# A memory tile moved from the router's stage to the end of the experts, and both norms there computed from one round of sums

## The reference

```python
h2 = modulate(x, norm2_g[l], sh2, sc2)
moe = hier_moe(h2.reshape(b * s, d), w_rg[l], b_rg[l], w_re[l], b_re[l],
               w1[l], w3[l], w2[l]).reshape(b, s, d)
x = x + g2[:, None, :] * moe
return rms_norm(x, norm_f_g)            # end of the first block
...
for i in range(DEPTH_2):                # the second block
    h = rms_norm_2(x, norm_w[i])
    ...                                 # GLA or S5 branch of h
    k, v = jnp.split(mem_n @ w_kv, 2, axis=-1)   # in memory_attention
```

## Time and profile before

| | us |
|---|---|
| median of 3 runs | 1678.35 |
| lowest, highest | 1676.72, 1678.55 |
| the profiled execution | 1676.78 |
| its span, first to last instruction | 1675.0 |
| PE busy in the span | 1566.1 (93%) |
| DVE busy | 578.7 (35%) |
| ACT busy | 321.9 (19%) |
| POOL busy | 54.0 (3%) |

### The profile page before, as it was taken

How to read it: one execution, slowest core, us unless ns; L and a number is a source line. 1 busy time by engine, 2 the same in 40 slices (tenths; PEclk the granted TensorE clock), 3 DMA queues, 4 the chain that set the end, 5 groups by cost and what they waited for, 6 DMA issues and landing times. The chain is left out here.

```text
span 1675.0 us, 20622 instructions
## 1 busy us (share of the span) xinstructions
PE 1566.1 (93%) x8428; PEld 917.0 (55%) x8428; DVE 578.7 (35%) x958; ACT 321.9 (19%) x547; POOL 54.0 (3%) x125
## 2 busy tenths in 40 slices
PE   5999998999999999994999999988999899699997
PEld 2485654444344444442445887547777775388843
DVE  2445323111111111113202111215999999720000
ACT  2222101111111111111200201003333343230000
POOL 0000000000000000000000000001111111000000
PEclk8999999999999999997999999998999999799999
DMA  9444647899999999993232242342333333124330
GB/s 402 169 157 188 257 200 318 339 422 422 422 422 422 422 422 422 422 410 130 107 144 101 101 151 101 146 156 94 146 114 113 115 148 129 63 101 151 151 151 25
DMA packets 46024, 371.59 MB, mean 222 GB/s; under 512 B 5888, under 2 KB 10368, under 8 KB 11408
## 3 DMA queue, kind: packets, MB, share of 16 engines
q1 hardware_dynamic: 45824, 369.75, 55.0%
q10 hardware_dynamic: 144, 1.05, 0.2%
HBM read 369.73 MB, written 1.05 MB: 221 GB/s over the span
## 5 line engine op out<-in xcount | busy, mean ns | idle before, releaser
L1228 PE MATMUL ps<-ring,x_gathered 128*64 128x512 f32 x1024 | 225.2, 592 | 0.9 <-DVE x_gathered L1296 0.9
L1911 PE MATMUL ps<-hT,ring 128*128 128x256 f32 x768 | 174.7, 386 | 1.9 <-PEq L113 1.9
L1416 PE MATMUL ps<-ring,zT 128*128 128x512 f32 x384 | 165.5, 592 | 0.0
L1911 PEld LDWEIGHTS ps<-hT,ring 128*128 128x128 f32 x768 | 146.0, 192 | 29.9 <-issue 10.4
L1228 PEld LDWEIGHTS ps<-ring,x_gathered 128*64 128x64 f32 x1024 | 73.6, 137 | 146.6 <-issue 146.6
L1305 DVE TENSOR_TENSOR act_slots<-gate,ps 64x512 f32<-64x512 f32 x32 | 22.1, 690 | 378.6 <-ACT gate L1267 378.6
L1416 PEld LDWEIGHTS ps<-ring,zT 128*128 128x128 f32 x384 | 72.9, 190 | 90.1 <-issue 89.9
L1251 PE MATMUL ps<-ring,act_turned 128*64 128x512 f32 x512 | 116.9, 598 | 0.0
L1529 PE MATMUL ps<-hT,ring 128*128 128x256 f32 x512 | 111.9, 380 | 0.0
L2086 PE MATMUL ps<-uT,ring 128*128 128x256 f32 x512 | 111.0, 379 | 0.0
L1529 PEld LDWEIGHTS ps<-hT,ring 128*128 128x128 f32 x512 | 96.8, 190 | 16.0 <-issue 3.1
(11 more groups left out here) (446 smaller groups left out, 1676.9 us busy)
## 6 DMA issues: line engine op xcount, KB each, us to landing
ring<-in_experts SPq DMA_DIRECT2D x192, 1024.0 KB, 15.8
ring<-in_weights SPq DMA_DIRECT2D x75, 2048.0 KB, 7.5
b_raw<-in_s_b SPq DMA_DIRECT2D x16, 128.0 KB, 7.4
c_raw<-in_s_c SPq DMA_DIRECT2D x16, 128.0 KB, 7.2
x<-in_x ACTq DMA_DIRECT2D x1, 1024.0 KB, 5.3
mix_room<-in_mem SPq DMA_DIRECT2D x1, 1024.0 KB, 17.2
rows_b_g<-in_rows SPq DMA_DIRECT2D x1, 1024.0 KB, 19.3
out<-x SPq DMA_DIRECT2D x2, 512.0 KB, 2.7
```

Source lines behind the costliest of these rows:

```text
L1228: last = pe.matmul(h_ps[rows, :], xg[:, f, :], w[:, kk, m, :], start=(f == 0), stop=(f == KD - 1))
L1416: last = pe.matmul(self.bank(n, t), self.zT[:, 8 * kb + kk, t * P:(t + 1) * P], w[:, kk, :], start=(first and kk == 0), stop=(self.ends(i) ...
L1911: last = pe.matmul(out[:, f, :], w[:, kk, (2 * h + f) * P:(2 * h + f + 1) * P], rhs[:, kk, :], start=(kk == 0), stop=(kk == KD - 1))
```

## The change

M3 leaves `FRONT` and the router's stage and becomes tile `T_END_FIRST` (24), the number that it had. It is loaded at the end of the experts, in front of the next layer's first two tiles, and its two halves are computed in `stage_first_end`: one and a half of them ahead of the transposes, the rest behind. ACT copies them to `vm` there. The next layer's third tile is now loaded in that layer. In the router's stage the second expert's tiles wait for A10, M2 and A11.

The end of the first block works by halves of 128 tokens, and DVE reads the experts' sum from PSUM. For each half DVE forms x and x times the first norm's gain (`xg`), ACT sums the squares of both, and POOL gets both factors from the two sums: with m = s/1024 + 1e-6, `keep_by` is 1/sqrt(m), and `turn_by` is 1/sqrt(sg/1024 + 1e-6 m), where sg is the sum of squares of `xg`. `xg` times `turn_by` is turned by PE for the next layer, `xg` times `keep_by` is the new x.

```diff
-         "O0", "O1", "M1", "A10", "M2", "A11", "M3")
+         "O0", "O1", "M1", "A10", "M2", "A11")
-T_GLA = len(FRONT)
+T_END_FIRST = len(FRONT)
+T_GLA = T_END_FIRST + 1
...
-        banks = TwoBanks(k, "route", "M10:act M11:act A10:act M20:act G10:dve M21:act A11:act M30:act G11:dve M31:act")
+        banks = TwoBanks(k, "route", "M10:act M11:act A10:act M20:act G10:dve M21:act A11:act G11:dve")
...
-                tile(TILE_OF["M3"])
                 at = ROWS["norm_f_g"][0]
                 sp.dma_start(a["norm_f"][:], k.dram["rows"][at:at + D].partition_broadcast(P)).then_inc(norm_f_in, 16)
-                for n in range(T_GLA - RING, T_GLA):
+                for n in range(T_END_FIRST - RING, T_END_FIRST):
...
                 ada_tile(k, banks, pe, 11, a["crep"])
-                half_tile(k, banks, pe, "M30", "tm", k.memT)
                 pe.wait_ge(chosen_ready, 1)
...
                 ada_row(k, banks, pe, 11, a["part"])
-                half_tile(k, banks, pe, "M31", "tm", k.memT)
...
-                take("M30", a["vm"][:, 0, 512:1024])
-                take("M31", a["vm"][:, 1, 512:1024])
...
-                for n in range(T_GLA, T_GLA + RING):
+                for n in range(T_END_FIRST, T_END_FIRST + RING):
...
                             last.then_inc(done, 1)
                 pe.wait_ge(y_ready, n_pass * N_EXP + 1)
                 for t in range(TT):
-                    last = scatter(1, t, stop=True)
-                last.then_inc(summed, 1)
+                    scatter(1, t, stop=True)
             @block.scalar
             def _(act):
...
                     dve.drain()
                     dve.tensor_scalar(a["rank"][:], a["rank"][:], -float(SLOTS), None, ALU.add)
                     dve.drain()
-                dve.wait_ge(summed, 1)
-                dve.tensor_copy(a["moe"].rearrange("p t (n c) -> p t n c", n=2), acc[:])
 def stage_first_end(k, a):
     with ExitStack() as ctx:
-        xn = k.sb("xn2", [P, TT, D], ctx=ctx)
-        stats = [k.sb(f"end_{s}", [P, TT], ctx=ctx) for s in ("ss_f", "rstd_f", "ss_g", "rstd_g")]
-        ss_f, rstd_f, ss_g, rstd_g = stats
-        x_ready, summed, rstd_ready, x_normed, scaled, turned = (
-            k.sem(s) for s in ("moe_added", "end_summed", "end_rstd_ready", "x_normed", "end_scaled", "end_turned"))
-        tps = k.ps[:, 0:4, :].rearrange("p b (f t) -> p (b f) t", f=2)
+        free = a["ring2"][:].rearrange("p r n -> p (r n)").rearrange("p (i t d) -> p i t d", t=TT, d=D)
+        moe, xg, xn, sq, sq_g = (free[:, i] for i in range(5))
+        ss, stat = k.sb("end_ss", [P, TT, 2], ctx=ctx), k.sb("end_stat", [P, TT, 5], ctx=ctx)
+        x_ready, xg_ready, summed, rstd_ready, scaled, turned, half_done, vm_out = (
+            k.sem(s) for s in ("moe_added", "x_gained", "end_summed", "end_rstd_ready", "end_scaled", "end_turned",
+                               "vm_half_done", "vm_half_out"))
+        acc = k.ps[:, 0:4, :].rearrange("p (t n) c -> p t (n c)", t=TT)
+        tps = k.ps[:, 0:4, :].rearrange("p (t b) (f c) -> p t b f c", t=TT, f=4)
         with k.nc.Block() as block:
             @block.vector
             def _(dve):
-                dve.tensor_tensor(a["moe"], a["moe"], bc(k.row("b_g2"), 1, TT), ALU.mult)
-                dve.drain()
-                dve.tensor_tensor(k.x[:], k.x[:], a["moe"], ALU.add).then_inc(x_ready, 1)
-                dve.wait_ge(rstd_ready, 1)
-                for t in range(TT):
-                    last = dve.scalar_tensor_tensor(out=k.x[:, t, :], in0=k.x[:, t, :], scalar=rstd_f[:, t:t + 1],
-                                                    in1=a["norm_f"][:], op0=ALU.mult, op1=ALU.mult)
-                last.then_inc(x_normed, 1)
-                dve.drain()
-                dve.wait_ge(rstd_ready, 2)
-                for t in range(TT):
-                    dve.tensor_scalar(xn[:, t, :], k.x[:, t, :], rstd_g[:, t:t + 1], None, ALU.mult).then_inc(scaled, 1)
+                for t in range(TT):
+                    dve.tensor_tensor(moe[:, t], acc[:, t], k.row("b_g2"), ALU.mult)
+                    dve.drain()
+                    dve.tensor_tensor(k.x[:, t], k.x[:, t], moe[:, t], ALU.add).then_inc(x_ready, 1)
+                    dve.drain()
+                    dve.tensor_tensor(xg[:, t], k.x[:, t], a["norm_f"][:], ALU.mult).then_inc(xg_ready, 1)
+                dve.drain()
+                for t in range(TT):
+                    dve.wait_ge(rstd_ready, t + 1)
+                    dve.tensor_scalar(xn[:, t], xg[:, t], stat[:, t, 3:4], None, ALU.mult).then_inc(scaled, 1)
                 gain = k.col("norm_w_2", 0, KD)
-                for f in range(KD):
-                    dve.wait_ge(turned, 2 * (f // 2) + 2)
-                    dve.tensor_scalar(k.hT[:, f, :], tps[:, f, :], gain[:, f:f + 1], None, ALU.mult)
+                for t in range(TT):
+                    dve.wait_ge(summed, 4)
+                    dve.tensor_scalar(k.x[:, t], xg[:, t], stat[:, t, 4:5], None, ALU.mult)
+                for t in range(TT):
+                    for b in range(2):
+                        dve.wait_ge(turned, 2 * t + b + 1)
+                        dve.tensor_tensor(k.hT[:, 4 * b:4 * b + 4, t * P:(t + 1) * P], tps[:, t, b],
+                                          bc(gain[:, 4 * b:4 * b + 4], 2, P), ALU.mult)
             @block.scalar
             def _(act):
-                for sem, ss in ((x_ready, ss_f), (x_normed, ss_g)):
-                    act.wait_ge(sem, 1)
-                    for t in range(TT):
-                        act.activation(xn[:, t, :], k.x[:, t, :], ACT.Square, accum_out=ss[:, t:t + 1]).then_inc(summed, 1)
+                for t in range(TT):
+                    for i, (sem, src, junk) in enumerate(((x_ready, k.x, sq), (xg_ready, xg, sq_g))):
+                        act.wait_ge(sem, t + 1)
+                        act.activation(junk[:, t], src[:, t], ACT.Square, accum_out=ss[:, t, i:i + 1]).then_inc(summed, 1)
+                for t in range(TT):
+                    act.wait_ge(*((half_done, 1) if t == 0 else (k.tile_done, T_END_FIRST + 1)))
+                    act.activation(a["vm"][:, t, 512:1024], k.ps[:, 6 + t, :], ACT.Copy).then_inc(vm_out, 1)
             @block.gpsimd
             def _(pool):
-                for i, (ss, rstd) in enumerate(((ss_f, rstd_f), (ss_g, rstd_g))):
-                    pool.wait_ge(summed, TT * (i + 1))
-                    rsqrt_mean(k, pool, rstd[:], ss[:], D).then_inc(rstd_ready, 1)
+                for t in range(TT):
+                    pool.wait_ge(summed, 2 * t + 1)
+                    mean, tiny, both, turn_by, keep_by = (stat[:, t, i:i + 1] for i in range(5))
+                    pool.tensor_scalar(mean, ss[:, t, 0:1], 1.0 / D, EPS, ALU.mult, ALU.add)
+                    pool.drain()
+                    pool.tensor_scalar(tiny, mean, EPS, None, ALU.mult)
+                    pool.tensor_tensor(out=keep_by, in0=mean, in1=k.c("minus_half")[:, 0:1], op=ALU.pow)
+                    pool.wait_ge(summed, 2 * t + 2)
+                    pool.tensor_scalar(both, ss[:, t, 1:2], 1.0 / D, None, ALU.mult)
+                    pool.drain()
+                    pool.tensor_tensor(both, both, tiny, ALU.add)
+                    pool.drain()
+                    pool.tensor_tensor(out=turn_by, in0=both, in1=k.c("minus_half")[:, 0:1], op=ALU.pow
+                                       ).then_inc(rstd_ready, 1)
             @block.tensor
             def _(pe):
-                pe.wait_ge(scaled, TT)
-                turn(k, pe, xn, KD, tps, turned)
+                k.wait_tile(pe, T_END_FIRST)
+                w = k.slot(T_END_FIRST)
+                def memory_half(t, kks):
+                    for kk in kks:
+                        last = pe.matmul(k.ps[:, 6 + t, :], k.memT[:, kk, t * P:(t + 1) * P], w[:, kk, :],
+                                         start=(kk == 0), stop=(kk == KD - 1), skip_group_check=True)
+                    return last
+                memory_half(0, range(KD)).then_inc(half_done, 1)
+                memory_half(1, range(KD // 2))
+                for t in range(TT):
+                    pe.wait_ge(scaled, t + 1)
+                    for f in range(KD):
+                        last = pe.transpose(tps[:, t, f // 4, f % 4], xn[:, t, f * P:(f + 1) * P], k.c("ident"))
+                        if f % 4 == 3:
+                            last.then_inc(turned, 1)
+                memory_half(1, range(KD // 2, KD)).then_inc(k.tile_done, 1)
 def first_block(k, a):
...
-                stream(k, sp, T_GLA, T_S5)
+                stream(k, sp, T_END_FIRST, T_S5)
```

More of the change, by code:

```diff
@@ L1142, in stage_experts @@
         names = ("expert_tile_done", "sel_ready", "xg_done", "xg_ready", "silu_done", "act_ready", "act_turned",
-                 "act_t_ready", "turn_begun", "selT_done", "selT_ready", "y_ready", "moe_zeroed", "moe_summed")
+                 "act_t_ready", "turn_begun", "selT_done", "selT_ready", "y_ready", "moe_zeroed")
```

(17 more changed lines are left out.)

## The result

The changed kernel takes 1660.59 us, median of 5 runs (1659.76 to 1665.38). The kernel before took 1678.55 beside it (1676.72 to 1683.32, 5 runs). Forecast were 1661 us.

What follows compares the result with a forecast made beforehand. The prediction took PE to bound the experts and summed -12.1 + 0.9 - 5.5 = -16.7 us, from 1676.78 to 1660.1 for the profiled execution, 1661 as a median. Its own range was 1656 to 1664, at 80%.

Steps and rivals of the forecast that it cites:

- What bounds: Expert stage: bound by PE at 14.42 us a step, with no wait for a DMA and the loads close behind.
- The router's stage, -12.14: Router's stage without M3's halves, copies and load: ends at 273.30 on DVE instead of 285.44 on ACT, -12.14 us.
- The clock there, +0.9: Start of the experts: PE idles about 6 us, and the lower clock slows zeroing and gather by +0.9 us, at most +1.97.
- The end of the experts, -5.5: Last scatter to next layer: M3 on PE hides the norms; next layer at 777.15 instead of 782.66, -5.5 us.
- The bound for a dearer evacuation: End of the experts: if a broadcast gain made DVE's four evacuations twice as dear, done at 776.8, +1.1 us.
- the rows' ratio of 1.4: End of the experts: POOL's first-half chain beside DVE grows by under 1 us, done before DVE is free at 766.6.
- The extreme case that I had priced: End of the experts: POOL stands still until 766.6, PE waits about 2 us; sum -14.7, time 1663.
- Rival 1: Expert stage: transfers bound it, so PE gains only 2.4 us instead of 11.2; time 1670; 5%.
- Rival 2: End of the experts: the clock falls under M3, 16 us are lost and nothing is gained; time 1677; 3%.
- Rival 3: End of the experts: M3's tile lands late, at 780.6, and PE's first instruction waits; +21.7 us, time 1683; 3%.
- Rival 4: Change of stage, or clock after the longer idle, costs 3 to 6 us more than taken: 1664 to 1667; 9%.
- The signs that I had named: Right: first L1203 product 11 to 13 us earlier, M3 directly behind last scatter. Wrong: DMA waits, PE waiting for scaled halves.

Runs made afterwards that it cites:

- after_again: The changed kernel itself, unaltered, run once more: 1664.36 us, ratio 0.9897 to the kernel before.
- pool_after: The changed kernel with POOL held at the end of the experts until DVE has issued all its sums: 1668.31 us, one execution.
- late_keep: The changed kernel with POOL's power for the write-back of x made one operation for both halves, behind the other powers: 1662.43 us, ratio 0.9897 to before.
- m3_clock: The kernel with M3 moved and the old norms, plus two unread PE products in the pause behind the end's transposes: 1667.68 us, ratio 0.9908 to before.
- m3_only: The kernel before with only M3 moved to the end of the experts, norms in their old order: 1670.08 us, ratio 0.9945 to before.
- m3_last: The changed kernel with M3's load issued third of the three tiles at the end of the experts, not first: 1674.86 us, one execution.
- pe_filler: The changed kernel with seven unread products added on PE behind its last one in the router's stage: 1665.93 us, ratio 0.9911 to before.

## Why the prediction was right, point by point

- **What bounds: right.** 464.3 us from the first expert product to the last scatter in twelve traces, whose experts start anywhere between 280.5 and 299.5.
- **The router's stage, -12.14: right.** PE starts the experts at 276.22, forecast 276.15, with A11 done 0.41 later. Between A11's end and PE's start the forecast had 8.15 and the trace has 7.81: DVE's end comes 5.33 after A11 (taken: 5.30), the change of stage 2.48 (taken: 2.85). That the DMAs there cost nothing is borne out by the same 464.3.
- **The clock there, +0.9: right in kind, its size is partly chance.** In the profiled execution zeroing and gather took 3.64 + 1.57 against 2.94 + 2.21 before: +0.06. In after_again they took 3.78 + 2.64: +1.27, and so, within 0.2, in four other traces with the same pause. Against full clock the lower level cost 1.59 here before the change and 1.65 to 2.86 after it; the pause grew from 3.48 to 5.57.
- **The end of the experts, -5.5: measured -4.81.** The last scatter ends 12.00 earlier than before, so 12 is added to the marks of after to read them in before's times. M3's tile was issued at 745.00 (taken: 744.8), landed 10.5 later (taken: 7.5) and was still 3.4 ahead of its use. PE is free at 770.34 (taken: 770.5). Then it waits 0.88 for DVE's second half, scaled at 770.41 in place of 769.2. The rest follows at nearly the forecast distances: next layer at 777.85 in place of 777.15. The bound for a dearer evacuation did not come: four took 2.47, 0.62 each.
- **The step that was mis-sized** is "By the rows' ratio of 1.4 the first half's chain grows by under 1 us and is still done before DVE is free". It compared the chain with DVE, but POOL itself has to be free for the second half, whose first sum is there at 754.39 (ACT's row ends then). A 128x1 operation took 1.25 and 1.14 us beside DVE's two-input sums and 0.22 and 0.19 without, a ratio of 5.7 and 6. The chain grew from 2.48 to 4.57, over twice the growth allowed for, and POOL was free at 755.29 (767.29 in before's times, when DVE had been free since 766.5); with DVE idle it would have been at about 753.3. So the second half's six operations began at 755.38, and only the last three of them should have been left when the last sum came, at 755.69; these three began at 757.11.
- **A term that was missing beside it.** Of that delay 0.56 stood nowhere in the forecast: the second half's first operation took 0.75 instead of 0.19 beside DVE's scaling of the first half, and it did so in pool_after (760.37) and late_keep (756.97) too. No run separates the two parts. The Trainium skill, "GPSIMD Engine Reference", Key points, named the right two engines and the right kind of instruction. This trace adds that the operation with a PSUM operand on DVE's side does no harm (POOL's 0.24 at 751.06 lies beside L1324, which reads PSUM), that with two SBUF inputs POOL's operation ends with DVE's, and that DVE's scaling, which reads one tensor from SBUF (0.75 for 128x1024, against 1.23 of a sum), holds POOL up just the same; in which mode DVE ran it no view here shows. The ratio I had came from 128x128 operations, 0.57 against 0.40. DVE's instructions beside them were short, 0.53 each (L1998, four in 2.10 from 1136.15), so the ratio does not carry over to DVE sums of 1.23. late_keep, which only shortens POOL's chain by one operation, took back 0.54 of the 0.88. The extreme case that I had priced (POOL standing still, PE waiting about 2) was not reached: PE waited 0.88, and the stage lost 0.70 against the forecast.
- **Rival 1, transfers bound the experts: refuted.** No DMA among PE's waits, no change in 464.3.
- **Rival 2, the clock falls under M3: refuted for the change** (10.54 for 24 products, 0.44 each, as at full clock), in all seven traces in which M3 starts 0.31 after the scatter. Where PE pauses 2.64 ahead of it, it can: M3's 32 take 15.43 in m3_clock, with the clock at 0.50 until 758, and 13.97 at full clock in m3_only after the same pause.
- **Rival 3, M3 late: didn't come, but its price is real.** m3_last pays 11.35 us in the stage, 3.0 of it by the clock.
- **Rival 4, 3 to 6 us more:** not in the profiled executions of the changed kernel, whose spans are 1658.6 and 1661.1. Between them the next layer's first half differs by 1.67 (8.78 against 7.11) and the experts' start by 1.21, two clock levels that fell out otherwise in the same instructions; the other stretches give 0.4 back. But of the eleven executions of the changed kernel five took 1665.24 to 1667.57, which is this rival's time or above it. They have no trace; the kernel before spreads as far beside it (1676.72 to 1685.13), so I can't say that the change made them so.
- **The total is in part luck.** The router's part gained 1.2 more than forecast (-12.40 against -11.24: the clock term was 0.8 too high and the change of stage 0.4 too long), the end 0.7 less, and the two stretches ahead of A11's end and behind the next layer's first product took 0.8 more; together -16.4 against -16.7. By after_again's trace the router's part is -11.19, and its median of 1664.36 lies just above the forecast's range of 1656 to 1664, though the ratio is the same, since the kernel before took 1681.06 beside it.
- **The signs that I had named:** PE's first scatter product 12.07 earlier and M3 directly behind the last scatter at full clock came true. One sign of being wrong came too, PE waiting 0.88 for the scaled second half, and with it the next layer starts 19.23 after the last scatter, not 18 to 19.

What I hadn't seen is what joins the two parts. M3 hides under the norms and costs 1.52 us in the stage, and for that PE stays busy and the next layer begins at full clock, in seven of the eight traces that have both parts. Alone, the norms give 0.35% (0.9953 to 0.9977) and M3's move 0.55% (0.9923 to 0.9966); together they give 1.1% (0.9 to 1.29), which by the intervals can't be told from the sum. In span each alone gives +2.4 and -6.7, against -16.4, but single spans carry some microseconds of chance.

Open: why the granted clock falls in some executions and not in others at the same pause of 2.10, and what sets the early part of a run (A11 ends between 268.0 and 273.0 in these twelve traces, where PE does the same work up to there).

## What to carry to other kernels

When work is moved out of one idle stretch into another, price each by the chain that ends it there, and then ask what PE's pause in front of the next long stage will be: filling a stretch in which PE would idle is worth the work hidden, plus the clock of what comes after where the pause would let it fall. A small operation on POOL that is put beside an SBUF operation of DVE such as these is to be priced at what that one has left to run (1.1 to 1.2 us beside a sum, 0.75 beside a scaling here), not by a ratio. And a tile that gates the first instruction of a stage belongs first in its queue; two tiles ahead of it cost 11 us here, with the clock.

## What the runs showed of the hardware that was not expected

- A POOL operation of 128x1 beside a DVE sum with two SBUF inputs ends with that sum: 1.25 and 1.14 us against 0.22 and 0.19 with DVE idle. Beside a DVE scaling of one SBUF tensor it does too: 0.75 against 0.19. Beside a DVE product that reads PSUM it loses nothing (0.24 at 751.06, 0.24 in pool_after with DVE idle).
- The granted clock fell in every pause of 5.57 us before the experts (seven traces). It also fell in pauses of PE of 2.10 (after_again), 2.46 (pe_filler), 2.64 (m3_clock, not in m3_only) and 3.41 us (m3_only), and did not in pauses of 1.69 and 1.73, nor in the same pause of 2.10 in seven other traces. The fall can also come after PE has begun again: 1.3 us after, behind waits of 0.46 and 1.98 (pool_after), and 0.9 us after, behind 3.48 (before). It cost 1.7 to 2.9 us in the following 16 products, and 1.6 to 2.9 in the zeroing and gather before the experts.
- Executions of one kernel lie up to 8 us apart (after_again: 1659.79 to 1667.57) with nothing in the program to tell them apart. Differences under 2 us had to be read from stretches of a trace, not from times.
